# A dense job set behind the state products in three passes of a scan, and two head copies set ahead of a row copy

## What is computed

```python
def step(state, inp):                       # hgrn2_scan, per head and direction
    qc, kc, vc, gc = inp
    bcum = jnp.cumsum(gc, axis=2)
    btot = bcum[:, :, -1:]
    qe = qc * jnp.exp(bcum)
    ke = kc * jnp.exp(-bcum)
    att = jnp.where(causal_in_chunk, jnp.einsum('bhtk,bhsk->bhts', qe, ke), 0.0)
    o = jnp.einsum('bhtk,bhkv->bhtv', qe, state) + jnp.einsum('bhts,bhsv->bhtv', att, vc)
    kd = kc * jnp.exp(btot - bcum)
    new_state = jnp.exp(btot)[:, :, 0, :, None] * state + jnp.einsum('bhsk,bhsv->bhkv', kd, vc)
    return new_state, o
...
o = o * lax.rsqrt(jnp.mean(o * o, axis=-1, keepdims=True) + EPS)      # _hg_readout, per head
```

## Time and profile before

| | |
|---|---|
| median of 3 runs | 1706.7 us (1698.45 to 1707.29) |
| the profiled execution | 1702.57 us, of which the span from first to last instruction is 1700.7 us |
| PE busy | 1589.7 us, 93% of the span |
| DVE, ACT busy | 1006.4 us (59%), 688.6 us (40%) |
| mean granted TensorE clock | 0.958 of full |

### The profile page before, as it was taken

The page is one execution under the profiler, slowest core; times in us unless marked ns, Lnnn a source line. Parts: engine busy times, 40 slices in busy tenths (PEclk is TensorE's granted clock), DMA queues, the critical chain, the costliest instruction groups (busy, mean ns, idle before and its releaser), DMA issues.

```text
span 1700.7 us, 29199 instructions
## 1 busy us (share of the span) xinstructions
PE 1589.7 (93%) x12110; PEld 1458.7 (86%) x12110; DVE 1006.4 (59%) x1406; ACT 688.6 (40%) x819; POOL 18.3 (1%) x40
## 2 busy tenths in 40 slices
PE   6989899999999899998699999898999989989997
PEld 6876699999787699998587776867999989989997
DVE  5484667666643466667554653445666666676665
ACT  5352444343433443434444541244434343344332
POOL 0000000000300000000000000000000000000000
PEclk9998899999999999999799997999999999999999
DMA  5332544545445735454125544402454535534541
GB/s 220 126 139 104 218 149 178 197 169 198 130 184 190 271 128 219 160 200 183 43 100 198 205 178 144 179 1 100 149 197 173 197 128 176 192 126 173 197 173 50
DMA packets 39490, 273.90 MB, mean 161 GB/s; under 512 B 4784, under 2 KB 5936, under 8 KB 6768
## 3 DMA queue, kind: packets, MB, share of 16 engines
q1 hardware_dynamic: 37296, 264.26, 42.5%
q0 software_dynamic: 1392, 5.77, 1.2%
q10 hardware_dynamic: 720, 2.68, 0.4%
HBM read 271.64 MB, written 1.05 MB: 160 GB/s over the span
## 4 chain that ended last, share of the span: by engine, by line
PE 87%; DVE 8%; ACT 3%; DMA 1%; issue 1%; DVEq 0%; ACTq 0%; SPq 0%
PE L L1495 55%; PE D L1495 14%; PE M L1572 3%; PE N L1580 2%; PE D L1616 2%; DVE wlo L828 2%; PE D L1619 1%; ACT whi L447 1%; PE N L1646 1%; PE M L1560 1%; PE N L1861 1%; DVE arena L905 1%; DVE var L857 1%; PE D L1634 1%; DMA raw<-in_units 1%
## 5 line engine op out<-in xcount | busy, mean ns | idle before, releaser
L1495 PE MATMUL L<-h_hi,whi 128*128 128x256 f32 (+1 forms) x2096 | 619.4, 296 | 40.1 <-DVE h_lo L877 17.8
L1495 PE MATMUL L<-h_lo,whi 128*128 128x256 f32 (+1 forms) x2096 | 612.9, 292 | 0.0
L1495 PE MATMUL L<-h_hi,wlo 128*128 128x256 f32 (+1 forms) x2096 | 612.2, 292 | 0.0
L1495 PEld LDWEIGHTS L<-h_hi,whi 128*128 128x128 f32 x2096 | 411.9, 197 | 56.3 <-issue 50.5
L1495 PEld LDWEIGHTS L<-h_lo,whi 128*128 128x128 f32 x2096 | 411.9, 197 | 3.9
L1495 PEld LDWEIGHTS L<-h_hi,wlo 128*128 128x128 f32 x2096 | 411.2, 196 | 4.2
L828 DVE TENSOR_TENSOR wlo<-raw,whi 128x2048 fp32r<-128x2048 f32 x107 | 244.8, 2290 | 96.1 <-ACT whi L447 95.8
L966 DVE TENSOR_TENSOR wlo<-raw,whi 128x2048 fp32r<-128x2048 f32 x96 | 219.9, 2290 | 113.3 <-ACT whi L555 113.3
L447 ACT ACTIVATE whi<-raw 128x2048 fp32r<-128x2048 f32 x107 | 203.0, 1906 | 139.7 <-PE L L1495 125.6
L1495 PE MATMUL D<-hd_hi,whi 128*128 128x256 f32 x704 | 199.5, 283 | 6.4 <-DVE hd_lo L992 6.4
L1495 PE MATMUL D<-hd_lo,whi 128*128 128x256 f32 x704 | 199.2, 283 | 0.0
(11 more groups left out here) (261 smaller groups left out, 1968.0 us busy)
## 6 DMA issues: line engine op xcount, KB each, us to landing
raw<-in_units SPq DMA_DIRECT2D x251, 1024.0 KB, 4.8
arena<-in_relx POOLq DMA_DIRECT2D x12, 128.0 KB, 5.0
arena<-in_nax POOLq DMA_DIRECT2D x1, 1536.0 KB, 6.6
t<-in_mem ACTq DMA_DIRECT2D x1, 1024.0 KB, 8.1
x<-in_x ACTq DMA_DIRECT2D x1, 1024.0 KB, 12.6
arena<-in_ctx POOLq DMA_DIRECT2D x1, 1024.0 KB, 5.5
out<-t SPq DMA_DIRECT2D x8, 128.0 KB, 2.0
arena<-in_relx POOLq DMA_DIRECT2D x12, 64.0 KB, 4.9
```

The lines of the kernel that those rows point to most:

```text
L1495: ins = mm(dst, w[a], h[b], start=start and n == 0, stop=stop and n == 2, skip_group_check=True)
```

## The change

Three edits that belong together, and one by itself. PE: in passes with one dense job that job stands behind the state products and the second `modulate`, where passes with two have their second. DVE: the store of that job moves with it to the iteration behind. ACT by itself: in even iterations the two reads of `N0` (with the wait for `hg_o`) stand ahead of the third row copy, where they stood behind the `whi` copies and sigmoids.

```diff
@@ ACT, behind the four Exps of iteration e
+                if e >= 2 and e % 2 == 0:
+                    h = e // 2 - 1
+                    act.wait_ge(R["hg_o"], e)
+                    A.activation(hf[1][:, h, 0:T], N0[:, 0:T], ACT.Copy).then_inc(R["hg_sq"], 1)
+                    A.activation(hf[0][:, h, 0:T], N0[:, 0:T], ACT.Square).then_inc(R["hg_sq"], 1)
                 if 0 < e <= 2 * HGH:
                     rows_out()
...
-                if e >= 2 and e % 2 == 0:
-                    h = e // 2 - 1
-                    act.wait_ge(R["hg_o"], e)
-                    A.activation(hf[1][:, h, 0:T], N0[:, 0:T], ACT.Copy).then_inc(R["hg_sq"], 1)
-                    A.activation(hf[0][:, h, 0:T], N0[:, 0:T], ACT.Square).then_inc(R["hg_sq"], 1)
@@ DVE
-                if 1 < i <= passes + 1 and len(H_BESIDE[i - 2]) == 2:
-                    store(H_BESIDE[i - 2][1])
+                if 1 < i <= passes + 1:
+                    store(H_BESIDE[i - 2][-1])
...
-                    store(H_BESIDE[i - 1][0])
+                    if len(H_BESIDE[i - 1]) == 2:
+                        store(H_BESIDE[i - 1][0])
                     states(i - 1)
@@ PE
                 modulate(H_ADA + 3 * e, e == 0)
-                job(H_BESIDE[e][0])
+                if len(H_BESIDE[e]) == 2:
+                    job(H_BESIDE[e][0])
...
                 modulate(H_ADA + 3 * e + 1)
-                if len(H_BESIDE[e]) == 2:
-                    job(H_BESIDE[e][1])
+                job(H_BESIDE[e][-1])
                 pe.wait_ge(R["hg_am"], e + 1)
                 pe.wait_ge(R["hg_st"], e + 1)
```

## The result

| | before | after |
|---|---|---|
| median of 20 runs | 1705.01 us (1698.45 to 1707.29) | 1709.18 us (19 of them 1705.38 to 1710.80, one 4703.48) |
| ratio | | 1.0031, 95% interval 1.0021 to 1.0040 |
| span of the profiled execution | 1700.7 us | 1707.1 us |
| mean granted clock | 0.958 | 0.959 |

The ratio leaves the one run of 4703.48 us out as a slow one. By it the changed kernel is 0.31% slower, which is 5.3 us, and 4.2 us by the two medians: within the 0.5% that were called no change, with an interval that excludes zero. The forecast was 1714, range 1704 to 1725.

A forecast was written before the change was run, and what follows sets the result against it. PE, busy 93% of the span, bounds the kernel, so its stops and slow clock count. Terms: -14.7 + 16.2 + 7.6 = +9.1 us; 1706.7 + 9.1 - 2.0 = 1713.8, forecast 1714 us, range 1704 to 1725.

The forecast's parts named there:

- The moved job: PE, passes 5 to 7: the dense job covers DVE's state updates, so three waits ahead of the output products go, -6.0 us.
- The clock behind those waits: PE, pass 6's output products to pass 7's: clock stays at 2.4 GHz once the waits go, -6.7 - 2.0 = -8.7 us.
- the sum of gains: Waits removed in passes 5 to 7 plus clock regained behind them: -14.7 us, bounds -6.0 and -16.4.
- the 1.7 us set aside for iteration 6: PE, 1006 to 1014: 1.7 us lost at half clock, not counted as a gain but inside iteration 6's 4.1 us stop.
- The reads: ACT, even iterations: head reads delay row copies and `wlo`, so PE stops +5.1, +4.4, +4.1, +2.6, sum +16.2 us.
- New half clock: PE behind the new stops: 3.1 us lost in iteration 2, 1.4 in 4, 3.1 in 6; +7.6 us, bounds 0 and 18.4.
- The first rival: Longer half clock: new stops leave PE at 1.2 GHz as in 1024 to 1042, 18.4 for 7.6, 1725 us; chance 0.16.
- balance: Freed stretches regain all 4.1 us in the median, new stops cost at most 1.7 us of clock each: 1708 us; chance 0.18.
- The table load: ACT's chain: load taken as 1.28 us without the skill page's 1.38 us drain, which would add some 6 us, so 1720.
- The rival "faster": ACT reaches the reads only after the output products, so rows are on time and only the moved job counts: 1692; chance 0.08.

The follow-up runs named there:

- the idle matmuls: Kernel before the change, with 14 matmuls of unused product ahead of each state-update wait in passes 5, 6 and 7, nothing moved; outputs wrong: 1693.96 us, ratio 0.9946.
- the kept-busy kernel: Changed kernel with 36, 54 and 36 matmuls of unused product in the stops ahead of the turn in passes 2, 4 and 6: 1705.78 us, ratio 1.0012.
- the weight copies go first: Changed kernel with ACT's `whi` copies of an even iteration put ahead of the head reads and their wait for `hg_o`: 1693.66 us, ratio 0.9938 to before.

## Why the prediction was right, point by point

- **The moved job: right.** The three waits are gone and nothing took their place, neither `s_kt` nor the store; the job alone, measured, is faster by 1.1%.
- **The clock behind those waits: right in place, and near in size.** Passes 6 and 7 run at 2.4 GHz up to the output products of pass 7. The term was -8.7, the sum of gains -14.7; the moved job alone gave -18.8, and 9.2 came without any wait shortened, by the idle matmuls. By the stages the moved job alone gains 15.3 up to the turn behind pass 7, where the sum has 14.7, or 16.4 with the 1.7 us set aside for iteration 6. The rest, 2.9 us, is the half clock behind that turn. Leaving it out was right for the changed kernel: its window 1060 to 1069, around the stop for `wlo`, still has 6.8 us at 1.2 GHz.
- **The reads: right, point by point.** With t0 1.71 us behind the start of L1862, as in the earlier trace rows (921.14 to 922.85), I gave from t0 to the second turn 8.2, 10.4 and 8.2 us and to the job behind iteration 8 5.3; the trace has 8.26, 10.47, 8.26 and 5.30. The first stops are 1.02 us, given as 1.2. The modulate behind the turn of iteration 4 was given as 10.9 and starts at 11.4, since that turn itself runs at 1.2 GHz (0.94 us between 982.39 and 983.33).
- **New half clock: right.** The term was 3.1 for each of three stops. The windows have 6.8, 10.1 and 6.8 us at 1.2 GHz; a part lies ahead of the turns at 929.08, 982.39 and 1028.12. What is lost while busy is read behind them: 9.68 us from the turn to the head sums in pass 2, where the kernel before needs 7.11 (925.97 to 933.08), and the kept-busy kernel gives 2.7, 3.1 and 2.7 for the three. So it is some 2.6 to 3.1 us each. The first rival, 6.7 for each, is refuted by the profile, and with it one half of "balance", 1.7 for each.
- **The table load: the trace agrees with the term used.** The load at 923.76 takes 1.28 us and the sigmoids start at 925.06, 0.02 behind its end; the second one ends at 927.50, and ACT had then 0.62 us to spare ahead of its Ln. The drain of 1.38 us that the Trainium skill gives in ScalarE: Activation LUTs, section What ACT_TABLE_LOAD costs, once behind each of the two loads, would have brought the Ln past 928.13, where its row is (927.50 + 2 x 1.38 = 930.3); it is not seen, and the 6 us that an estimate put on it did not come.
- **The rival "faster" is refuted.** ACT is at the reads far ahead of time, 14.92, 14.45, 8.42 and 11.08 us in iterations 2, 4, 6 and 8; in the kernel before it stood idle ahead of them in iteration 2 alone, 3.42 us. The rival's own condition, stops and clock under 14.7 us together, is missed by the 24.0 us that they cost.
- **The size of the whole.** The forecast was +7.3 on the median; the ratio gives +5.3 and the two medians +4.2. In the profiled pair it is +6.4 against +9.1: 1.6 of the 2.7 us is pass 1's clock, of which the last section tells and which neither edit touches, 0.5 lies ahead of it, 0.3 behind the scan, and only 0.4 in the terms of the sum, whose errors nearly cancel. Another 1.7 us of the 4.8 by which 1714 is too high are in the median of three runs, 1706.7, which is 1705.0 over twenty. The other half of "balance", that the whole difference between median and profiled execution goes, fits the runs: over twenty runs it is 2.4 us before and 0.2 after. The forecast let half of 4.1 go, and no trace shows in which stretches the rest lay.

What stays open: how the 9.4 us that remain when the weight copies go first divide between stops and clock, why the reads alone cost only 15.9 us over the runs, and how much of the gain belongs to the clock in a given execution, since its stretches are not the same twice.

## What to carry to other kernels

A wait put into an engine's program holds everything that stands behind it on that engine, and what other engines derive from it: ask not what the moved instruction costs (two reads of 0.28 us each) but what was done in the idle time ahead of its old place. A change of two edits that comes out at zero should be run as two kernels; here one was worth 1.1% and the other took all of it back. And a stop costs more than its length on TensorE: work that is put into it is worth the wait plus the time at 1.2 GHz behind it, while a stop that falls into time already slow costs less (3.0 in place of 5.2 us behind pass 7). How long an engine waits doesn't tell what a stop costs; the time between two fixed points of the program does.

## What the runs showed of the hardware that was not expected

- The same wait, in the same program place, is followed by very different clocks. The load wait ahead of the stretch 898 to 908.5 (2.76 us before, 2.35 after) is followed by (1 - 0.67) x 2 x 10.5 = 6.9 us at 1.2 GHz in the one execution and by 3.4 us in the other, with nothing changed up to there. Nor does the wait's length decide: it is 2.80 us with the reads alone and 2.86 with the weight copies first, and from the end of it to the second modulate's turn PE takes 11.5 us in the one and 10.3 in the other. The kernel before spreads over 8.8 us from run to run, with no wait changed.
- After a stop of 1.02 us behind the output products, which are short matmuls, the clock is down in the kernel with the fillers (922.32, 1.83 us for a modulate), and up in the changed kernel (16 matmuls from 922.54 in 1.04 us). In the kernel before with its waits filled, the clock fell in pass 6 though the wait left there was 0.43 us, at 1023.09, and stayed up behind one of 1.48 us at 1009.64.
